# A hybrid decoder layer: AZ as the plain first projection, AV as a seven-product quad, heads of seven blocks

## The chip, the cores and the metric

The kernel runs on one NeuronCore of a Trainium2 chip. The metric is the device time of one execution in microseconds (us). Engines are TensorE (PE; PEld is its weight load), VectorE (DVE), ScalarE (ACT) and SyncE (SP), which here only issues DMAs. GpSimd is not used.

## What is computed

One layer over 512 tokens of width 2048, all in float32:

```python
h = rmsnorm(x, norm_g)
parts = split(h @ w_in)            # w_in: 2048 x 24576 columns in blocks of 1024, and three gates of 2048
aq, ak, av, az = parts[0:4]        # branch A, 8 heads of 2 x 64
# branch A: per head p = softmax(q1 k1) - lam * softmax(q2 k2), o = p @ v, rmsnorm(o)
ya = oa * silu(az)
# branch B: 8 heads, three groups (q, k, v each) with dilation 1, 4, 16, joined by their denominators
yb = ob * silu(bz)
yc = cb * conv3(cc * cx) * silu(cz)
merged = sum(sigmoid(gate_i) * (y_i @ w_branch_i))
out = rmsnorm(x + merged @ w_out, final_g)
```

A product is made in float32 precision by three matmuls: both operands are split into a high part, rounded to the fast format (fp32r), and the rest, and high x high, high x low and low x high are summed in PSUM (`three`, L619).

## The kernel before

**Units and splits.** Weights come in units of 128 x 1024 floats (512 KB). A unit's `w_hi` is made by ScalarE (a copy) and its `w_lo` by VectorE (a subtraction), each in a ring of three (`RING`). TensorE waits for `w_lo` (`lo_done`); ScalarE splits unit n+3 when TensorE has finished unit n (`pe_used`). SyncE loads the raw units into another ring of three.

**Stages in order.** (1) A *plain* projection of 1024 columns, 16 units, with activations held still and weights moving: the values of branch A (AV). (2) Five *quads*, 1 to 5. A quad is a block of 1024 columns by 2048 rows computed with seven products of halves (Strassen's scheme) instead of eight, P1 to P4 in 28 units of 12 matmuls. VectorE adds the halves of the weights (four kinds, `add_units`, four units each) and takes each product's two PSUM banks into `gin` (`take_g`); ScalarE stores the result to `c_dram`. These quads give AQ, AK and the three V of branch B. (3) Eight *heads*, with attention. (4) Quads 6 to 15, branch C and gates, with branch C's convolution beside them. (5) The three branch projections and the output projection, also with seven products, from summed weights in `s_dram`.

**Heads.** Head 0 and head 7 are written out, heads 1 to 6 are a loop of three heads that runs twice (`Fori`, on each engine). A head has eight projection blocks, w = 2 to 9: Q0, K0, Q1, K1, Q2, K2, AZ, BZ. Each is 128 columns, two units of 24 matmuls (8 chunks of K x 3), with weights held still. The result lies in one of three banks `proj`, and VectorE scales it by the tokens' root (`scale_block`). AQ and AK of the head come from `c_dram` and are turned by TensorE into such a bank. Between the units, TensorE does attention: `scores_a`, `scores_b` (into `sc_ps`), `probs_a`, `probs_b` (transposes into `tr_ps`), `values_a`, `values_b` (into `o_ps`) and `squares_a` (sum of squares for branch A's norm). A step of softmax goes through the engines: scores (PE), `bias` with the minimum (DVE), `exps` (ACT), `norm` (DVE), `probs` (PE), `turned` (high part ACT, low part DVE). Branch A has four such steps in a head (0 to 3), branch B four (0 to 3), of which B's last three fall into the next head's first blocks.

**Sums of branch weights.** 24 times within the heads, ScalarE loads 2 MB of branch or output weights into `ssum` (`load_sums`), VectorE makes four additions (`sum_units`), ScalarE stores 2 MB to `s_dram` (`store_sums`). There is one buffer, so a load waits for the store before. `SUMS_FIRST` and `SUMS_LOOP` give the units at which they are loaded; the sum is two units later, the store three.

**What sets the order.** Everything is written out by hand: each engine's program calls the same steps in its own order, in `blocks` (PE), two functions `head` (ACT and DVE) and the loops over quads. Every engine takes its instructions in order, so a wait holds up all behind it.

```python
def bank(self, b):
    return (NBLK1 * self.k + ENTRY[b]) % RING
```

## Time and profile before

| | |
|---|---|
| time, median of 3 runs (lowest, highest) | 2504.5 us (2504.45, 2504.55) |
| the profiled execution's own time | 2505.15 us |
| its span, first to last instruction | 2503.4 us |
| mean granted clock of TensorE | 0.999 |
| busy: PE, PEld, DVE, ACT | 2484.4, 2053.7, 1945.7, 1069.8 us |
| matmuls | 11454 |
| read from and written to HBM | 420.64 MB, 96.47 MB |

Busy time is the union of an engine's instructions. Matmuls overlap, so the printed mean of one is longer than the distance between two starts. "Idle before, releaser" is the time in which an engine did nothing before an instruction, and what the profile takes to have ended it; "issue" means that it waited for nothing the profile shows. Times in timelines are counted from the first instruction.

### The profile page before, as it was taken

How to read it: one execution, taken by the hardware profiler on the slowest of the kernel's cores; microseconds unless marked ns; L12 is line 12 of the kernel's file. 1: busy time of each engine (PE TensorE's matmuls, PEld its weight loads, DVE VectorE, ACT ScalarE, POOL GpSimd, SP SyncE). 2: the span in 40 equal slices, each digit the busy share in tenths (PEclk: the TensorE clock that was granted, in tenths of full speed). 3: DMA queues.
4: the chain of work that ended last, by engine and by line, in shares of the span. 5: the costliest groups of instructions: out<-in, count | busy, mean ns of one | idle time of the engine just before them, and what ended most of it. 6: DMA issues, size and time to landing. Idle time of an engine off the chain costs nothing.

```text
span 2503.4 us, 30481 instructions
## 1 busy us (share of the span) xinstructions
PE 2484.4 (99%) x11454; PEld 2053.7 (82%) x11454; DVE 1945.7 (78%) x2266; ACT 1069.8 (43%) x1329; POOL 0.2 (0%) x4
## 2 busy tenths in 40 slices
PE   9999999999999999999999999999999999999998
PEld 8888888888888888888887788888878888788887
DVE  8797788566676767767678887788878888898875
ACT  5343333334333333333434433344444445655644
POOL 0000000000000000000000000000000000000000
PEclk9999999999999999999999999999999999999999
DMA  8255444686776667766535545445565456787666
GB/s 317 95 198 188 150 133 143 203 301 214 252 266 231 223 213 248 264 234 225 191 106 193 203 168 193 170 154 193 181 218 203 160 197 219 261 286 247 226 227 202
DMA packets 184902, 519.15 MB, mean 207 GB/s; under 512 B 14129, under 2 KB 59442, under 8 KB 181042
## 3 DMA queue, kind: packets, MB, share of 16 engines
q1 hardware_dynamic: 87872, 342.62, 39.9%
q10 hardware_dynamic: 96882, 174.55, 19.8%
q8 instruction: 94, 1.54, 0.2%
q14 instruction: 54, 0.44, 0.1%
HBM read 420.64 MB, written 96.47 MB: 207 GB/s over the span
## 4 chain that ended last, share of the span: by engine, by line
PE 92%; DVE 3%; DMA 3%; ACT 1%; issue 1%; DVEq 0%; ACTq 0%
PE proj L621 13%; PE proj L623 13%; PE proj L622 13%; PE sc_ps L621 6%; PE sc_ps L622 6%; PE sc_ps L623 6%; PE tr_ps L621 6%; PE tr_ps L622 6%; PE tr_ps L623 6%; PE o_ps L622 4%; PE o_ps L623 4%; PE o_ps L621 4%; PE tr_ps L664 1%; DVE w_lo L1547 1%; DMA rows<-c_dram 1%; DMA raw<-s_dram 1%
## 5 line engine op out<-in xcount | busy, mean ns | idle before, releaser
L1008 ACT ACTIVATE w_hi<-raw 128x1024 fp32r<-128x1024 f32 x296 | 314.0, 1061 | 430.3 <-PE proj L623 138.1
L1008 ACT ACTIVATE w_hi<-kb 128x1024 fp32r<-128x1024 f32 x280 | 297.2, 1062 | 442.6 <-PE proj L623 156.9
L1547 DVE TENSOR_TENSOR w_lo<-raw,w_hi 128x1024 fp32r<-128x1024 f32 x296 | 361.2, 1223 | 156.2 <-ACT w_hi L1008 155.3
L1547 DVE TENSOR_TENSOR w_lo<-kb,w_hi 128x1024 fp32r<-128x1024 f32 x280 | 342.7, 1224 | 116.6 <-ACT w_hi L1008 116.0
L621 PE MATMUL proj<-act_hi,w_hi 128*128 128x512 f32 x1024 | 405.8, 396 | 1.7 <-DVE w_lo L1591 1.7
L623 PE MATMUL proj<-act_hi,w_lo 128*128 128x512 f32 x1024 | 399.6, 390 | 0.0
L622 PE MATMUL proj<-act_lo,w_hi 128*128 128x512 f32 x1024 | 398.7, 389 | 0.0
L1057 ACT ACTIVATE w_hi<-raw 128x1024 fp32r<-128x1024 f32 x128 | 135.6, 1060 | 344.8 <-PE proj L623 339.9
L1591 DVE TENSOR_TENSOR w_lo<-raw,w_hi 128x1024 fp32r<-128x1024 f32 x128 | 156.6, 1224 | 103.1 <-ACT w_hi L1057 102.6
L623 PEld LDWEIGHTS proj<-act_hi,w_lo 128*128 128x128 f32 x1024 | 192.2, 188 | 41.3
L621 PEld LDWEIGHTS proj<-act_hi,w_hi 128*128 128x128 f32 x1024 | 192.8, 188 | 40.2 <-DVE w_lo L1591 1.9
L622 PEld LDWEIGHTS proj<-act_lo,w_hi 128*128 128x128 f32 x1024 | 192.6, 188 | 38.2
L621 PE MATMUL sc_ps<-w_hi,act_hi 128*128 128x512 f32 x360 | 141.2, 392 | 0.6 <-DVE w_lo L1547 0.5
L621 PE MATMUL tr_ps<-w_hi,act_hi 128*128 128x512 f32 x360 | 140.8, 391 | 0.8 <-DVE w_lo L1547 0.8
L622 PE MATMUL sc_ps<-w_lo,act_hi 128*128 128x512 f32 x360 | 140.2, 389 | 0.0
L622 PE MATMUL tr_ps<-w_lo,act_hi 128*128 128x512 f32 x360 | 140.1, 389 | 0.0
L623 PE MATMUL sc_ps<-w_hi,act_lo 128*128 128x512 f32 x336 | 130.8, 389 | 0.0
L623 PE MATMUL tr_ps<-w_hi,act_lo 128*128 128x512 f32 x336 | 130.8, 389 | 0.0
L621 PE MATMUL tr_ps<-w_hi,tb 128*128 128x512 f32 x328 | 128.4, 392 | 0.6 <-DVE w_lo L1547 0.6
L623 PE MATMUL tr_ps<-w_hi,tb 128*128 128x512 f32 x328 | 127.7, 389 | 0.0
L622 PE MATMUL tr_ps<-w_lo,tb 128*128 128x512 f32 x328 | 127.7, 389 | 0.0
L621 PE MATMUL sc_ps<-w_hi,tb 128*128 128x512 f32 x272 | 106.5, 392 | 1.9 <-DVE w_lo L1547 1.7
(310 smaller groups left out, 4765.1 us busy)
## 6 DMA issues: line engine op xcount, KB each, us to landing
raw<-wg SPq DMA_DIRECT2D x128, 512.0 KB, 3.9
raw<-wst SPq DMA_DIRECT2D x128, 512.0 KB, 4.9
kb<-wg SPq DMA_DIRECT2D x28, 2048.0 KB, 7.6
ssum<-ws ACTq DMA_DIRECT2D x24, 2048.0 KB, 9.3
s_dram<-ssum ACTq DMA_DIRECT2D x24, 2048.0 KB, 7.7
raw<-s_dram SPq DMA_DIRECT2D x96, 512.0 KB, 4.4
raw<-ws SPq DMA_DIRECT2D x72, 512.0 KB, 4.1
kb<-wg SPq DMA_DIRECT2D x56, 512.0 KB, 6.3
```

What stands on the lines that cost most here:

```text
L621: nc.tensor.matmul(out, w_h, a_h, start=first, stop=False, skip_group_check=shared)
L622: nc.tensor.matmul(out, w_h, a_l, start=False, stop=False, skip_group_check=shared)
L623: return nc.tensor.matmul(out, w_l, a_h, start=False, stop=last, skip_group_check=shared)
L664: end = nc.tensor.transpose(tr_ps[idx % 2][:, n * P:(n + 1) * P], tile, ident[:, :])
L1008: nc.scalar.activation(w_hi[r % RING][:, :], src, ACT.Copy).then_inc(hi_done, 1)
L1057: nc.scalar.activation(w_hi[slot][:, :], raw[x][:, :], ACT.Copy).then_inc(hi_done, 1)
L1547: tt(w_lo[r % RING][:, :], src, w_hi[r % RING][:, :].bitcast(f32), ALU.subtract).then_inc(lo_done, 1)
L1591: tt(w_lo[slot][:, :], raw[x][:, :], w_hi[slot][:, :].bitcast(f32), ALU.subtract).then_inc(lo_done, 1)
```

## The change

- The plain projection now computes AZ. Its operands are swapped: weights held still, activations moving, so that a bank holds 128 columns by 512 tokens, the form of a head. It is stored unscaled, one bank per head, to a new `z_dram`, and each head loads its own (`load_z`) into `z_a` and scales it (`scale_z`) in block K2.
- AV becomes one more quad. There are six quads (1 to 6) ahead of the heads, and 7 to 16 behind.
- A head has seven blocks (w = 2 to 8: Q0, K0, Q1, K1, Q2, K2, BZ), 14 units.
- The attention steps move. Scores and transposes now mostly stand between the two units of a block on TensorE, and the transposes of a step come one block after its scores. ScalarE's and VectorE's parts follow. `values_b` of a head stays at the end of K1 in the next head, with `scores_a(1)` ahead and `probs_a(0)` behind it.
- In the last head, steps 2 and 3 of branch B move into the quad after the heads (number 7); that quad uses `o_ps`, `proj0` for the Z chain and `sc_ps` for Y; `values_b` goes to `sc_ps0`, and ScalarE copies `o_ps` to `o_a`.
- Sums of branch weights: one moves into quad 6; in the heads one every four units, with the sum at the end of a block and behind its softmax work.

The core of the diff:

```diff
-NBLK1, NHU1 = 10, 16
+NBLK1, NHU1 = 9, 14
-QUADS_V, QUADS_C, QUADS_G, QUADS_O = 6, 10, 16, 2
+QUADS_V, QUADS_C, QUADS_G, QUADS_O = 7, 11, 17, 2
-SUMS_FIRST = (0, 4, 8, 12)
-SUMS_LOOP = (2, 6, 12, 16, 20, 24, 28, 34, 40, 44)
+SUMS_QUAD, SUM_QUAD_AT = 9, (13, 14, 15, 16)
+SUMS_FIRST = (1, 5, 9)
+SUMS_LOOP = (1, 5, 9, 13, 17, 21, 25, 29, 33, 37)
...
 plain_quad, PE:
-                            ts = slice(P * b, P * (b + 1))
-                            end = three(plain[half][b][:, :], act_hi[:, k, ts], act_lo[:, k, ts], w_hi[slot][:, cs], w_lo[slot][:, cs],
+                            ws = slice(C * kk + P * b, C * kk + P * (b + 1))
+                            end = three(plain[half][b][:, :], w_hi[slot][:, ws], w_lo[slot][:, ws], act_hi[:, k, :], act_lo[:, k, :],
...
 blocks, PE, between the two units of block w:
+                    if w < 5 and not fresh:
+                        scores_b(i - 1, w - 1)
+                    if w == 5:
+                        scores_a(i, 0)
+                    if 6 <= w < 8:
+                        scores_a(i, w - 4)
+                    if w == BZ:
+                        scores_b(i, 0)
+                    if w < 6 and not fresh:
+                        probs_b(i - 1, w - 2)
+                    if 6 <= w:
+                        probs_a(i, w - 5)
                     pe.wait_ge(lo_done, NHU1 * i + (R_H + t + 2))
                     multiply(h.bank(w), h.slot(t + 1), act_hi, act_lo, 8, False, True)
...
+                    if w == 5:
+                        scores_a(i, 1)
+                        if not fresh:
+                            values_b(i - 1, o_ps, (o_free, 2 * i))
+                        probs_a(i, 0)
+                    if w == BZ:
+                        values_a(i)
                         if last:
-                            scores_b(i, 2)
-                        else:
-                            values_a(i)
                             scores_b(i, 1)
                             probs_b(i, 0)
...
 head, DVE, between the two units of block w (behind split(t)), the end of K2 and the end of a block:
+                    if w == BZ:
+                        bias_b(i, 0)
+                        turned_a(i, 3)
+                        low_v(2 * i + 1, v_a)
+                        silu(i, 0, AZ)
+                        norm_b(i, 0)
...
                     scale_block(h, w)
+                    if w == 7:
+                        scale_z(i)
                     split(t + 1)
...
+                    m = h.sums(t + 1, SUM_AT)
+                    if m is not None:
+                        sum_units(m)
...
 after the heads, PE:
                         if n == 1:
-                            scaled(HEADS - 1, AZ)
+                            scaled(HEADS - 1, Q2)
                             squares_a(HEADS - 1, pb[0])
-                            scores_b(HEADS - 1, 3)
+                        if n in (1, 3):
+                            scores_b(HEADS - 1, (n + 3) // 2)
                         if n in (1, 3, 5):
                             probs_b(HEADS - 1, (n + 1) // 2)
                         if n == 7:
-                            values_b(HEADS - 1)
+                            values_b(HEADS - 1, sc_ps[0], (biased, 8 * HEADS + 1))
```

How the instructions stand on VectorE, in head 0, from the end of block K2 on. Before, K2's two units (`w_lo`) close the step 3 of branch A, and the low part of the values (`v_lo`) stands in the block behind, AZ, ahead of everything but one `w_lo`; BZ is still to come:

```order
L1728 SCALAR_TENSOR_TENSOR pr<-sc,rsum,tmp_a 128x512
L1591 TENSOR_TENSOR w_lo<-raw,w_hi 128x1024
L1786 TENSOR_TENSOR v_lo<-v_a,v_hi 128x512
L1704 TENSOR_TENSOR z_a<-proj,rstd 128x512
L1591 TENSOR_TENSOR w_lo<-raw,w_hi 128x1024
L1743 ISA sc,low<-masks,sc_ps 128x512
L1743 ISA low 128x1
L1745 ISA sc,nmax<-masks,sc_ps,low 128x256
L1745 ISA nmax 128x1
L1756 TENSOR_TENSOR pt_lo<-tr_ps,pt_hi 128x4x128
```

Now (from the gate's scaling at the end of K2 into BZ):

```order
L1739 TENSOR_TENSOR z_a<-z_a,rstd 128x512
L1620 TENSOR_TENSOR w_lo<-raw,w_hi 128x1024
L1604 TENSOR_TENSOR ssum<-ssum 128x1024
L1606 TENSOR_TENSOR ssum<-ssum 128x1024
L1608 TENSOR_TENSOR ssum<-ssum 128x1024
L1610 TENSOR_TENSOR ssum<-ssum 128x1024
L1620 TENSOR_TENSOR w_lo<-raw,w_hi 128x1024
L1776 ISA sc,low<-masks,sc_ps 128x512
L1776 ISA low 128x1
L1778 ISA sc,nmax<-masks,sc_ps,low 128x256
L1778 ISA nmax 128x1
L1789 TENSOR_TENSOR pt_lo<-tr_ps,pt_hi 128x4x128
```

The next row there is `v_lo<-v_a,v_hi`: the low part of the values has moved behind the sum of weights, the bias and the transposed probabilities, in the same block at whose end TensorE asks for it.

VectorE in the quad after the heads, units 5 and 6 (each begins with its `w_lo`), before:

```order
L1547 TENSOR_TENSOR w_lo<-raw,w_hi 128x1024
L1756 TENSOR_TENSOR pt_lo<-tr_ps,pt_hi 128x4x128
L1750 RECIPROCAL rsum<-sums 128x1
L1751 TENSOR_SCALAR pr<-sc,rsum 128x768
L1547 TENSOR_TENSOR w_lo<-raw,w_hi 128x1024
L1790 RECIPROCAL tmp_a<-tmp_a 128x512
L1793 SCALAR_TENSOR_TENSOR o_a<-o_ps,gsub,tmp_a 128x512
L1893 TENSOR_SCALAR gin<-proj,rcol 128x512 x2
```

And now:

```order
L1567 TENSOR_TENSOR w_lo<-raw,w_hi 128x1024
L1776 ISA sc,low<-masks,sc_ps 128x512
L1776 ISA low 128x1
L1778 ISA sc,nmax<-masks,sc_ps,low 128x256
L1778 ISA nmax 128x1
L1789 TENSOR_TENSOR pt_lo<-tr_ps,pt_hi 128x4x128
L1783 RECIPROCAL rsum<-sums 128x1
L1784 TENSOR_SCALAR pr<-sc,rsum 128x768
L1567 TENSOR_TENSOR w_lo<-raw,w_hi 128x1024
L1823 RECIPROCAL tmp_a<-tmp_a 128x512
L1830 SCALAR_TENSOR_TENSOR o_a<-o_a,gsub,tmp_a 128x512
L1931 TENSOR_SCALAR gin<-proj,rcol 128x512 x2
```

The bias of step 3 of branch B (two instructions and their minima) has moved from unit 3 to unit 5, ahead of the reciprocal.

## Rows read from the trace of the kernel before

**Rows 1.** The page: busy time, and the granted clock in 40 slices.
```profile
span 2503.4 us, 30481 instructions
PE 2484.4 (99%) x11454; PEld 2053.7 (82%) x11454; DVE 1945.7 (78%) x2266; ACT 1069.8 (43%) x1329; POOL 0.2 (0%) x4
PEclk9999999999999999999999999999999999999999
```

**Rows 2.** One quad: stretch, its length, busy (instructions) per engine, PEclk, DMA share, GB/s.
```profile
200.00:276.20 76.20, 76.20 (x338) 63.13 (x337) 61.53 (x59) 29.77 (x29) 0.00 (x0) 1.00 0.48 165
```

**Rows 3.** The same view, two looped heads.
```profile
580.00:685.40 105.40, 105.40 (x522) 87.51 (x521) 71.45 (x114) 39.70 (x66) 0.00 (x0) 1.00 0.65 228
685.40:790.80 105.40, 105.40 (x522) 87.50 (x521) 74.93 (x115) 38.36 (x65) 0.00 (x0) 1.00 0.73 262
```

**Rows 4.** Timeline of TensorE: quad 5 into head 0; scores of branch B.
```profile
471.64 0.39 PE L621 MATMUL o_ps<-w_hi,tb 128*128 128x512 f32 x1
...
479.80 0.39 PE L621 MATMUL proj<-act_hi,w_hi 128*128 128x512 f32 x1
...
1300.95 0.48 PE L621 MATMUL sc_ps<-qk_hi 128*128 128x512 f32 x1
...
1302.10 0.47 PE L621 MATMUL proj<-act_hi,w_hi 128*128 128x512 f32 x1
```

**Rows 5.** Chain that ended last: `values_b` in four successive heads (start, length).
```profile
732.76 1.78 PE o_ps L712 x16
838.13 1.78 PE o_ps L712 x16
...
945.47 1.78 PE o_ps L712 x16
1050.85 1.78 PE o_ps L712 x16
```

**Rows 6.** Timelines around the loop's jump: TensorE, VectorE, ScalarE.
```profile
892.69 0.82 PE L664 MATMUL tr_ps<-ident,pr 128*128 128x128 f32 x6
895.23 0.49 PE L621 MATMUL proj<-act_hi,w_hi 128*128 128x512 f32 x1 [1.71 <-DVE w_lo L1591]
...
878.43 1.22 DVE L1591 TENSOR_TENSOR w_lo<-raw,w_hi 128x1024 fp32r<-128x1024 f32 x1 [0.40 <-ACT w_hi L1057]
...
902.99 1.06 ACT L1057 ACTIVATE w_hi<-raw 128x1024 fp32r<-128x1024 f32 x1 [4.49 <-issue]
```

**Rows 7.** The sums' loads and stores: ScalarE's timeline, landing (L1042, then L1046), waits.
```profile
866.75 0.40 ACTq L1046 DMA_DIRECT2D s_dram<-ssum  x1
...
874.86 0.41 ACTq L1042 DMA_DIRECT2D ssum<-ws  x1
...
DMA to landing us min/median/max: 8.3/9.3/13.3
...
DMA to landing us min/median/max: 7.0/7.7/9.9
...
DVE ssum L1583 <- DMA ssum<-ws: 4.7, 5, 1.2
```

**Rows 8.** VectorE's groups: count, busy, mean ns of one.
```profile
L1702 DVE TENSOR_TENSOR qk<-proj,rstd 128x512 f32<-128x512 f32 x32 | 34.4, 1075 | 23.4 <-PE proj L623 22.5
L1584 DVE TENSOR_TENSOR ssum<-ssum 128x1024 f32<-128x1024 f32 x24 | 29.4, 1225 | 0.8
L1743 DVE CUSTOM_DVE_ANT_0 sc<-masks,sc_ps 128x512 f32<-128x512 f32 x32 | 21.8, 681 | 0.3 <-DVE pr L1751 0.3
L1745 DVE CUSTOM_DVE_ANT_0 sc<-masks,sc_ps,low 128x256 f32<-128x256 f32 x32 | 15.4, 481 | 6.1 <-DVE low L1743 6.1
```

**Rows 9.** Timelines in quad 6, unit 7: VectorE, then TensorE.
```profile
1336.11 3.35 DVE L1790 RECIPROCAL tmp_a<-tmp_a 128x512 f32<-128x512 f32 x1
...
1341.47 1.22 DVE L1547 TENSOR_TENSOR w_lo<-raw,w_hi 128x1024 fp32r<-128x1024 f32 x1
...
1342.74 0.50 PE L621 MATMUL sc_ps<-w_hi,tb 128*128 128x512 f32 x1 [1.68 <-DVE w_lo L1547]
```

More of the change, by code:

```diff
@@ L708, in values_b @@
                 pe.wait_ge(vg_in, 32 * i + 32)
-                pe.wait_ge(o_free, 2 * i + 2)
+                pe.wait_ge(*free)
                 for g in (1, 2):
                     for c in range(4):
-                        nc.tensor.matmul(o_ps[:, c * P:(c + 1) * P], v_g[g][:, c, :], pt_g[:, g - 1, c, :],
+                        nc.tensor.matmul(bank[:, c * P:(c + 1) * P], v_g[g][:, c, :], pt_g[:, g - 1, c, :],
                                          start=g == 1 and c == 0, stop=False)
@@ L716, in values_b @@
                     bs = slice(32 * n, min(32 * n + 64, P))
-                    end = three(as_class(o_ps[:, :])[:, :, bs], v_hi[:, n, :], v_lo[:, n, :], pt_b[0][:, n, :, bs],
+                    end = three(as_class(bank[:, :])[:, :, bs], v_hi[:, n, :], v_lo[:, n, :], pt_b[0][:, n, :, bs],
                                 pt_b[1][:, n, :, bs], False, n == 3)
@@ L1143, in squares_o @@
                 nc.scalar.activation(sq_hi[:, :], o_ps[:, :], ACT.Square).then_inc(sq_ready, 1)
+                if last:
+                    nc.scalar.activation(o_a[:, :], o_ps[:, :], ACT.Copy).then_inc(o_free, 1)
             def root_o(i, bank):
@@ L1177, in head @@
                         comb_high(6, t2[0], f2, (comb_sum, 6))
-                    if last and w == 9:
-                        squares_o(i)
-                        turned_b(i, 0)
+                    if w < 6 and not fresh:
+                        turned_b(i - 1, w - 2)
+                    if w < 5 and not fresh:
+                        exps_b(i - 1, w - 1)
+                    if 6 <= w:
+                        turned_a(i, w - 5)
+                    if w == 5:
+                        exps_a(i, 0)
+                    if 6 <= w < 8:
+                        exps_a(i, w - 4)
+                    if w == BZ:
+                        exps_b(i, 0)
+                    m = h.sums(t, SAVE_AT)
+                    if m is not None:
+                        store_sums(m)
                     split(t + 1)
@@ L1183, in head @@
                         store_gate(QUADS_V - 1, 2)
+                    if w == 3 and not fresh:
+                        act.wait_ge(vb_in, 16 * i)
+                        act.wait_ge(o_ready, 2 * i - 1)
+                        high_v(v_b)
                     if w == 4:
+                        for b in SPLIT:
+                            split_block(i, b)
                         if fresh:
@@ L1829, in head @@
                         low_turn(h, AQ)
+                        if not fresh:
+                            low_squares(i - 1)
                     if w == K0:
                         low_turn(h, AK)
+                    if w < 5 and not fresh:
+                        bias_b(i - 1, w - 1)
+                        turned_b(i - 1, w - 2)
+                        if w == 4:
+                            inverse_a(i - 1)
+                            norm_o(i - 1)
+                        norm_b(i - 1, w - 1)
@@ new lines, in head @@
+                    if fresh and w == 4:
+                        for n in range(8):
+                            dve.wait_ge(g_stored[n], 16 * QUADS_V)
+                    if w == 5:
+                        bias_a(i, 0, fresh)
+                        if not fresh:
+                            turned_b(i - 1, 3)
+                        norm_a(i, 0)
+                    if 6 <= w < 8:
+                        bias_a(i, w - 4, fresh)
+                        turned_a(i, w - 5)
+                        if w == 6 and not fresh:
+                            join_b(i - 1, o_ps)
+                        norm_a(i, w - 4)
@@ L1841, in head @@
-                    if w == 6 and not fresh:
-                        join_b(i - 1)
-                    if w == 8:
-                        low_v(2 * i + 1, v_a)
-                    if w == 9:
-                        silu(i, 0, AZ)
-                    if last and w == 9:
-                        turned_b(i, 0)
-                        bias_b(i, 1)
                     scale_block(h, w)
+                    if w == 7:
+                        scale_z(i)
                     split(t + 1)
-                    if w < 4 and not fresh:
-                        bias_b(i - 1, w)
@@ new lines, in head @@
+                    if w == 5:
+                        bias_a(i, 1, fresh)
+                        turned_a(i, 0)
+                        if not fresh:
+                            join_a(i - 1)
+                            silu(i - 1, 1, BZ)
+                        norm_a(i, 1)
+                    if last and w == BZ:
+                        bias_b(i, 1)
+                        turned_b(i, 0)
+                        low_squares(i)
+                        norm_b(i, 1)
+                    m = h.sums(t + 1, SUM_AT)
@@ L1875, in take_g @@
+                    if m is not None:
+                        sum_units(m)
             def take_g(q, p):
@@ L1948, in take_plain @@
                 dve.wait_ge(pe_used, RING + UNITS_V // 2 * (half + 1))
[L1949 removed]
+                nc.vector.tensor_copy(gin[:, 4 * half + b, :], plain[half][b][:, :]).then_inc(got, 1)
             def sums_of(q, n):
@@ L2016, in _ @@
             head(fixed(0))
-            links = 3 * (steps["n"] - before - 2 * len(SUMS_FIRST) + 6) + 2 * len(SUMS_LOOP)
+            links = 3 * (steps["n"] - before - 2 * len(SUMS_FIRST) + 7) + 2 * len(SUMS_LOOP)
             with dve.Fori(0, 2) as j:
```

239 lines of the change are left out of this document (100 added, 139 removed).

## The prediction

> **What bounds the kernel now.** I read the page first, then stretches, then single instructions. The page [rows 1] shows TensorE busy 99% of a span of 2503.4 us, its granted clock in the top digit throughout (the 2.4 GHz level), and VectorE at 78%. So TensorE's list of matmuls is the time, and other engines matter only where they make it wait. Stretches of pure projection and of attention differ. A seven-product quad lasts 76.2 us, in which TensorE never idles and VectorE works 61.5 us [rows 2]. A looped head lasts 105.4 us, again without idle TensorE, with VectorE at 71 to 75 us [rows 3]. Some 19 us of the span are idle TensorE (2503.4 less 2484.4).
>
> Matmuls overlap, so the 0.39 us printed for one is not its price; the distance between starts is. In a quad 36 of 128x512 start in 471.64 to 479.80, 0.2267 us each [rows 4], and the change of form there, from activations held still to weights held still, leaves no gap. The same rows print equal durations on both sides. That is the price of every such matmul here: an 8-chunk half block (24) costs 5.44 us, a quad (7 products x 16 x 3 = 336) 76.2 us, as rows 2 measure.
>
> **The sum of the matmuls.** AZ as a head block cost 16 x 3 = 48 matmuls in each of eight heads, 384. It becomes the plain first projection, which is 16 units of 24, 384 too, and takes the slot that AV had. AV now costs a quad, 336. Net 48 fewer: 48 x 0.2267 = **10.9 us less**. In place: eight heads lose 10.9 us each (87.1), one quad adds 76.2. The attention matmuls, transposes and their breaks keep their number. A head should last 105.37 - 10.88 = 94.5 us (period from [rows 5]).
>
> **Work that goes beside it.** The quad adds 28 splits where 16 go, 16 weight additions of about 1.22 us and 7 evictions of two banks on VectorE. The 61.5 us of [rows 2] hold all of these, so they lie in a 76.2 us quad with 14.7 us of VectorE spare: zero; the four additions of a branch-weight sum (4.8 us, [rows 8]) that move into the last quad before the heads fit too, since that quad prepares no successor. Without that spare the 4.8 us would be the price. The plain projection's evictions become copies of the same size: zero. The swapped operands: zero by rows 4. SyncE's weight ring keeps its rule, three units ahead: zero. The gate's load and scaling (one 128x512, under 1.1 us by the scaling of [rows 8]) replace one eviction per head: zero, hidden by the head's spare 20 us of VectorE. The load is one DMA of 256 KB more per head on ScalarE's queue, ahead of a sum's load; it counts below.
>
> **The jump of the loop.** The heads' loop runs three heads twice. The head period is 105.37 us but 107.34 across its jump [rows 5]: 1.97 us. The profile names the residual split (w_lo) as releaser. I don't believe it: TensorE's last transposes start at 892.69, it resumes at 895.23, while the unit it resumes with had its w_lo at 878.43 plus 1.2; and ScalarE, at 902.99, has 4.5 us in which it waited for nothing shown [rows 6]. So I take the gap as the jump itself and leave it: zero, with -2.0 as the other end (were it VectorE's lateness, the new order would remove it) and nothing above, since the number of jumps is the same. The Trainium skill (Runtime: NRT & Kernel Launch, Instruction fetch mechanics) says that a taken branch to a page outside the fetch window has to fetch it before going on. By that rule the 2 us stay and the sum below is 2496.3; by the profile's releaser they would go, and it were 2494.3. The trace agrees with the rule as far as one jump can.
>
> **The tight place in a head.** Softmax steps now stand in mid-block, each a block from the next (first pair of pieces of the order). After its scores (1.15 us, [rows 4]) a step needs a bias of 0.7 + 0.5 [rows 8], an exp and a scaling, each near 1 us, and a w_lo or two stand between: some 6 us, where the transposes ask for it 12 us later. That holds. What doesn't hold so well is block BZ after a block K2 whose end carries a weight sum (sums stand at the end of every second block; in heads 0, 1, 3, 4 and 6 one is at the end of K2). From the end of K2, VectorE: scaling K2 1.0 and the gate 0.6, w_lo 1.1 (from 1.6 on), the sum 4.8, w_lo 1.1, bias 1.3, transposed probabilities 0.6, low part of v_a 0.6: 11.3 us with the small waits. TensorE asks for that low part at the end of BZ, 5.44 + 1.15 + 0.35 + 5.44 = 12.4 us. Slack 1.1 us, if the sum's data are in. That depends on the sum before, at the end of K1: VectorE's small steps there take about 7.4 us and the sum 4.8, of which 4.4 lie beside TensorE's attention, so it ends 7.8 us into Q2; w_lo, bias and exp follow (3.5), and the store goes out at 11.3 of Q2's 12.4 us. It lands 7.7 later, ScalarE issues the next load at once (866.75 and 874.86 show that distance), and that lands after 9.3 [rows 7]: with K2's 12.7 us gone, 3.6 us into BZ, where VectorE is ready at 2.8. So the slack falls to 0.3 us. One load took 13.3 and one store 9.9; with both a head stalls 4.0 + 2.2 - 0.3 = 5.9 us. Ends: 0 and 5.9 us per head. The medians give no stall and a part of the loads is later, so I take 0.3 for each of five heads, **+1.5 us**, close to the medians of rows 7. ScalarE meanwhile waits for the store with the next split queued behind it, 1.2 us late against three units of lead: nothing. Elsewhere (Q1, where the 3.35 us reciprocal [rows 9] meets a sum in heads 2 and 5) I count a surplus of about 3.5 us against some 8 us that the ring of three units gives: zero, at most 1.4 each.
>
> **The seam to the seventh quad.** Here before, TensorE lost 1.7 us: the reciprocal (3.35), the normalization and two evictions ran before w_lo of unit 7 at 1341.47 [rows 9]. The change puts scores and bias 3 between units 3 and 5 instead of earlier. TensorE then reaches unit 7 later by 1.2 us (scores), the reciprocal starts about 2.2 later (bias 1.3 plus the exp chain behind it): **+1.1 us**, ends 0 and 2.5. The second pair of pieces of the order shows what stands ahead of that reciprocal. The new copy of o_ps on ScalarE is under 1 us, hidden by the four units before P5; if not, it costs itself. The rest of that quad rests on the same transfers: zero.
>
> **Sum.** The profiled execution took 2505.15 us, span 2503.4 and 1.75 around it; it lies 0.65 above the median of the three runs. 2505.15 - 10.9 + 0 + 1.5 + 1.1 = 2496.9; against the median 2504.5 - 8.2 = **2496.3 us**, 0.33% less. The measurement can tell about 0.2% (5 us) from no change.
>
> **Rivals.**
> 1. *All of it arrives.* The load lands by its median, the slacks hold, the seam costs nothing: 2504.5 - 10.9 = 2493.6, with the jump's gap gone 2491.6. For: TensorE was never idle in a looped head but at the jump. Against: VectorE already waited for these loads five times [rows 7], when the need was no earlier than now. Chance 0.33.
> 2. *The weight sums become the wait (the slower side).* Mechanism: at the end of K2 VectorE, in order, stands at the sum for its load, and the low part of v_a is queued behind it. A head stalls by what store and load together exceed 17.3 us (7.7 + 9.3 + 0.3). At 2.0 us per head the gain is gone (5 x 2.0 + 1.1), at 3.0 the kernel is 5 us slower; with every load at 13.3 us it is 3.7 per head, 18.5 in all: 2504.5 - 10.9 + 18.5 + 1.1 = 2513.2. For: loads are now issued behind more work, beside y_a, v_b and the gate's load. Against: only a few of 24 loads can have been near 13.3. Chance 0.07 of slower, and 0.15 that it or an overfull VectorE takes 4 to 14 us and leaves 2499.5 to 2509.5 (within 0.2%).
> 3. *The new quad isn't free.* VectorE's spare there is used up by the moved sum: at most 4.8 us, 2501.1. Rows 2 speak against it; inside the 0.15.
>
> **Numbers.** Forecast (2494 to 2499.5) 0.45; all of it 0.33; within 0.2% 0.15; slower 0.07. Faster 0.78, same 0.15, slower 0.07. Range: the low end takes most of rival 1 (the full saving, 0.6 below it for errors in my small terms, not the jump's 2), 2493; the high end takes half of the middle case, 2501.5.
>
> **What the new profile would show.** Quads and plain units as before, 76.2 us each, heads starting 76.2 us later; looped heads 94.5 us apart, plus up to 1 where a sum ends K2; about 2 us more across the jump, which decides between my reading and w_lo; a gap of 2.5 to 3 us before unit 7 of the seventh quad. I am wrong if quads 1 to 6 show idle TensorE, if heads are over 96.5 us apart, or if values of branch A (o_ps) wait for v_lo by more than 1 us in a head. Should the heads be 94.5 with no waits, rival 1 has it.

## The result, and the profile after

The change makes the kernel slower: 2524.7 us (median of 4, 2521.1 to 2525.9) against 2504.5 of the kernel before in the same job (4 runs), ratio 1.0078, 95% interval 1.0066 to 1.0091. The forecast was 2496.3, in a range of 2493.0 to 2501.5.

The page of the changed kernel (its profiled execution took 2524.84 us), against [rows 1]:

```profile
span 2522.9 us, 30435 instructions
PE 2484.2 (98%) x11406; PEld 2049.8 (81%) x11406; DVE 1981.1 (79%) x2308; ACT 1082.6 (43%) x1342; POOL 0.2 (0%) x4
```

The 48 matmuls are gone (11454 to 11406), but TensorE's busy time is the same (2484.4, now 2484.2) and its idle time has doubled, from 19.0 to 38.7 us. The same stretch of one quad as in [rows 2]:

```profile
200.00:276.20 76.20, 76.20 (x338) 63.13 (x337) 61.55 (x60) 29.72 (x28) 0.00 (x0) 1.00 0.48 166
```

It is as before: TensorE is never idle in these 76.2 us. The chain that ended last shows where the time goes: `values_b` in successive heads (start, length), as [rows 5].

```profile
697.96 1.98 PE o_ps L716 x16
...
893.15 1.98 PE o_ps L716 x16
...
996.03 1.98 PE o_ps L716 x16
...
1095.82 2.05 PE o_ps L716 x16
...
1193.01 1.98 PE o_ps L716 x16
...
1289.03 1.98 PE o_ps L716 x16
```

Two heads take 195.2 us, then one 102.9 (across the jump), 99.8, 97.2 and 96.0, where 94.5 was forecast. Waits of ScalarE, VectorE and TensorE in the changed kernel (us in total, times, longest):

```profile
ACT w_hi L1065 <- DMA s_dram<-ssum: 65.0, 13, 6.8
ACT L1163 <- DMA s_dram<-ssum: 10.4, 2, 5.3
DVE ssum L1604 <- DMA ssum<-ws: 9.7, 7, 2.6
PE o_ps L625 <- DVE v_lo L1819: 7.5, 5, 3.1
PE proj L647 <- ACT tmp_a L1163: 4.9, 2, 2.5
PE proj L625 <- issue: 3.9, 1, 3.9
PE o_ps L625 <- DVE pt_lo L1789: 1.9, 1, 1.9
```

The four rows of PE are 18.2 us of new idle time in looped and first heads (only the jump's 1.7 was there before). Behind some of the gaps the granted clock came down. Windows of 4 us around the jump and around the 3.1 us gap (columns as in [rows 2]):

```profile
936.00:940.00 4.00, 0.67 (x7) 0.53 (x5) 1.67 (x2) 1.09 (x2) 0.00 (x0) 0.98 1.04 389
940.00:944.00 4.00, 3.47 (x8) 2.81 (x9) 0.00 (x0) 0.00 (x0) 0.00 (x0) 0.50 0.61 200
944.00:948.00 4.00, 4.00 (x13) 3.11 (x13) 0.00 (x0) 0.00 (x0) 0.00 (x0) 0.67 0.00 0
...
1036.00:1040.00 4.00, 0.90 (x4) 0.50 (x3) 3.77 (x9) 1.82 (x3) 0.00 (x0) 0.85 0.46 136
1040.00:1044.00 4.00, 4.00 (x18) 3.60 (x17) 2.50 (x4) 1.25 (x3) 0.00 (x0) 0.72 1.00 409
```

PEclk 0.50 is the 1.2 GHz level; matmuls start 0.43 us apart there instead of 0.23. Over the nine such windows of the changed kernel before its end the missing clock, (1 - PEclk) x 4 us each, is 8.6 us, which counts as busy time. The kernel before has none, except at its very end. So the account is -10.9 (matmuls) + 16.5 (gaps in the heads) + 1.0 (seam) + 8.6 (clock) = 15.2 of the 19.5 us by which the span grew. Of the other 4.3, 2.2 are idle time outside these rows (idle time grew by 19.7 in all) and 2.1 are busy time; what that busy time is was not worked out.

### The profile page after: what moved, and what is told of

It reads as the page before. It is cut to its first block, busy times and chain, and to the rows that moved or that the text cites. A ratio compares the mean times of both kernels' runs of the same rounds, so it can differ in the third digit from the quotient of the medians.

```text
span 2522.9 us, 30435 instructions
## 1 busy us (share of the span) xinstructions
PE 2484.2 (98%) x11406; PEld 2049.8 (81%) x11406; DVE 1981.1 (79%) x2308; ACT 1082.6 (43%) x1342; POOL 0.2 (0%) x4
## 4 chain that ended last, share of the span: by engine, by line
PE 79%; DMA 9%; DVE 8%; issue 3%; ACT 1%; ACTq 0%; DVEq 0%
PE proj L625 9%; PE proj L627 8%; PE proj L626 8%; PE sc_ps L625 7%; PE sc_ps L626 6%; PE sc_ps L627 6%; PE tr_ps L625 6%; PE tr_ps L626 6%; PE tr_ps L627 6%; PE o_ps L625 4%; PE o_ps L626 4%; PE o_ps L627 4%; DMA s_dram<-ssum 4%; DMA ssum<-ws 3%; DVE w_lo L1567 1%
## 5 line engine op out<-in xcount | busy, mean ns | idle before, releaser
L1016 ACT ACTIVATE w_hi<-kb 128x1024 fp32r<-128x1024 f32 x300 | 318.1, 1061 | 474.1 <-PE proj L627 162.3
L1567 DVE TENSOR_TENSOR w_lo<-kb,w_hi 128x1024 fp32r<-128x1024 f32 x300 | 366.9, 1223 | 122.5 <-ACT w_hi L1016 121.9
L625 PE MATMUL proj<-act_hi,w_hi 128*128 128x512 f32 x944 | 376.3, 399 | 3.9 <-issue 3.9
L627 PE MATMUL proj<-act_hi,w_lo 128*128 128x512 f32 x944 | 369.9, 392 | 0.0
L626 PE MATMUL proj<-act_lo,w_hi 128*128 128x512 f32 x944 | 369.4, 391 | 0.0
L625 PEld LDWEIGHTS proj<-act_hi,w_hi 128*128 128x128 f32 x944 | 178.6, 189 | 39.1 <-issue 4.0
L627 PEld LDWEIGHTS proj<-act_hi,w_lo 128*128 128x128 f32 x944 | 178.1, 189 | 38.4
L626 PEld LDWEIGHTS proj<-act_lo,w_hi 128*128 128x128 f32 x944 | 178.6, 189 | 35.4
L625 PE MATMUL tr_ps<-w_hi,tb 128*128 128x512 f32 x344 | 134.4, 391 | 0.0
L627 PE MATMUL tr_ps<-w_hi,tb 128*128 128x512 f32 x344 | 134.0, 390 | 0.0
L1089 ACT ACTIVATE sc<-sc,nmax 128x768 f32<-128x768 f32 (+4 forms) x96 | 65.5, 683 | 119.1 <-DVE nmax L1778 59.9
```

The costliest lines, as they stand in the source:

```text
L625: nc.tensor.matmul(out, w_h, a_h, start=first, stop=False, skip_group_check=shared)
L626: nc.tensor.matmul(out, w_h, a_l, start=False, stop=False, skip_group_check=shared)
L627: return nc.tensor.matmul(out, w_l, a_h, start=False, stop=last, skip_group_check=shared)
L1016: nc.scalar.activation(w_hi[r % RING][:, :], src, ACT.Copy).then_inc(hi_done, 1)
L1089: end = nc.scalar.activation(tile[:, lo:hi], tile[:, lo:hi], ACT.Exp, scale=-1.0, bias=nmax[:, m:m + 1], accum_out=sums[:, m:m + 1])
L1567: tt(w_lo[r % RING][:, :], src, w_hi[r % RING][:, :].bitcast(f32), ALU.subtract).then_inc(lo_done, 1)
```

## How one head goes wrong

The head with the longest gap, around the end of K2. ScalarE's store and load of a sum:

```profile
1009.98 0.40 ACTq L1054 DMA_DIRECT2D s_dram<-ssum  x1
...
1018.73 0.39 ACTq L1050 DMA_DIRECT2D ssum<-ws  x1
```

VectorE, from the split that waited for ScalarE to the low part of the values:

```profile
1020.34 1.23 DVE L1620 TENSOR_TENSOR w_lo<-raw,w_hi 128x1024 fp32r<-128x1024 f32 x1 [5.87 <-ACT w_hi L1065]
1021.48 0.68 DVE L1751 CUSTOM_DVE_ANT_0 sc<-masks,sc_ps 128x512 f32<-128x512 f32 x1
...
1027.52 1.22 DVE L1620 TENSOR_TENSOR w_lo<-raw,w_hi 128x1024 fp32r<-128x1024 f32 x1
1030.84 1.23 DVE L1604 TENSOR_TENSOR ssum<-ssum 128x1024 f32<-128x1024 f32 x1 [2.10 <-DMA ssum<-ws]
...
1038.67 0.68 DVE L1819 TENSOR_TENSOR v_lo<-v_a,v_hi 128x512 fp32r<-128x512 f32 x1
```

TensorE:

```profile
1035.92 0.39 PE L627 MATMUL proj<-act_hi,w_lo 128*128 128x512 f32 x1
1039.40 0.80 PE L625 MATMUL o_ps<-pt_hi,v_hi 128*128 128x512 f32 x1 [3.10 <-DVE v_lo L1819]
```

The forecast had the store out 11.3 us into Q2, which is 1010.1 here, counted back from the values' due time: right (1009.98). The load follows 8.75 later (the forecast's timeline took 8.1, its rule 7.7), and its data are in at 1030.84, 12.1 after its issue (9.3 was taken). The forecast's rule, a stall of what store and load together exceed 17.3 us, gives 8.75 + 12.1 - 17.3 = 3.6; TensorE waited 3.1. In the three other looped heads with a sum there it gives 1.4 to 2.0 and TensorE waited 1.0 to 1.2. In the whole kernel the landings are these, of the loads and of the stores (min, median, max; [rows 7] had 9.3 and 7.7):

```profile
DMA to landing us min/median/max: 7.8/9.6/12.7
...
DMA to landing us min/median/max: 7.0/8.5/11.2
```

The second thing to see is the first row of VectorE. ScalarE stood for the store's landing until 1018.73, with the copy w_hi of the next unit behind it; so w_lo came 5.9 us later than VectorE was free, and the bias of the softmax step stands behind w_lo. TensorE didn't need that unit yet. VectorE's order made the bias need it. In this head that delay was made up (VectorE stood idle for the load afterwards, 2.10 us). In head 2, where no sum stands at the end of K2, it reached TensorE by itself:

```profile
831.02 1.06 ACT L1065 ACTIVATE w_hi<-raw 128x1024 fp32r<-128x1024 f32 x1 [2.26 <-DMA s_dram<-ssum]
...
832.11 1.23 DVE L1620 TENSOR_TENSOR w_lo<-raw,w_hi 128x1024 fp32r<-128x1024 f32 x1 [4.54 <-ACT w_hi L1065]
...
835.88 0.50 PE L625 MATMUL o_ps<-pt_hi,v_hi 128*128 128x512 f32 x1 [1.08 <-DVE v_lo L1819]
```

In head 0 (TensorE's wait of 1.9 us on `pt_lo`) VectorE didn't wait for the sum's load either; one w_lo in K2 had made it stand 5.2 us for ScalarE, whose copy came behind the store's landing (2.1 us in q1_own_queue, where ScalarE has no store to wait for).

## Experiments

**The sums left out, whole or in part.** Three kernels from the changed one, one from the kernel before. The stage behind reads unsummed weights of the same size in all of them (in e3_transfers_only what was stored back unsummed).

```diff
 e1_no_sums, b1_no_sums:
             def load_sums(m):
+                return
             def store_sums(m):
+                return
-                for step in range(4):
-                    sum_unit(m, step)
 e1_no_sums, b1_no_sums, e2_adds_only:
-                load_ring(x, (s_dram if summed_ else ws)[i, kind, :, :])
+                load_ring(x, ws[i, kind, :, :])
 e2_adds_only, in the heads:
-                        load_sums(m)
-                        store_sums(m)
 e3_transfers_only, in the heads:
-                for step in range(4):
-                    sum_unit(m, step)
+                dve.wait_ge(osum_in, 16 * (m + 1))
+                dve.sem_inc(osum_done, 1)
```

> The changed kernel without the 24 sums of branch and output weights: their loads, additions and stores are left out, and the projections behind read the unsummed weights in the same amount. Kernel before 2504.5 us, changed kernel 2524.7 us. Theory S (the sums are what stalls TensorE in the seven-block heads, and the lowered clock follows from those stalls): the six waits of branch A's values at the end of BZ and the two for the root at K0 vanish, the only gaps left are the loop's jump and the seam after the heads, mean granted clock 0.999; 2504.5 - 10.9 + 1 for the seam, 2493 to 2498 us. Rival T (the new order of attention is too tight by itself): gaps before branch A's values stay at 1 us or more per head, at least 2508 us. Rival Q (the added quad or the swapped projection cost): time lost before 557 us, not seen so far, at least 2504 us.

Measured: 2494.9 (2492.2 to 2500.6), ratio 0.9968 (0.9956 to 0.9979). The sums are the whole loss: without them the change brings 9.1 us of the 10.9. The chain's rows of `values_b`:

```profile
692.67 1.98 PE o_ps L716 x16
...
787.18 1.98 PE o_ps L716 x16
...
881.69 1.98 PE o_ps L716 x16
...
977.02 1.98 PE o_ps L716 x16
...
1071.54 1.98 PE o_ps L716 x16
```

94.51 us per head, as forecast, and 95.33 across the jump.

> The changed kernel with all additions of the sums on VectorE at their places, but with one load and one store in the last quad only: the 23 transfers within the heads are left out, and the additions repeat on the same data. Theory S1 (the round trip store, load, sum through one buffer is what is late, through ScalarE's wait for the store and VectorE's wait for the load): gaps before branch A's values below 0.3 us each, as in the kernel without sums, 2494 to 2500 us. Rival S2 (the 4.8 us of additions in VectorE's queue are late by themselves): the gaps of about 1 us before branch A's values stay, the waits for the root vanish, 2503 to 2512 us.

Measured: 2497.0, 0.9973 (0.9963 to 0.9984). VectorE does every addition, 1983.1 us busy, and TensorE waits for none of them. VectorE isn't overfull.

> The changed kernel with all loads and stores of the sums and all their waits on both engines, but without the additions in the heads (23 x 4 instructions on VectorE are left out). Theory S1: the round trip loses its 4.8 us of additions and 3 to 4 us of waiting, so store and load fit in two blocks; between the kernel without sums and the changed kernel, 2495 to 2503 us, with ScalarE still waiting for stores. Theory S2: the same as without sums, 2493 to 2498 us. If the waits for transfers alone hold everything up (theory S3), 2510 us or more and gaps before the values as in the changed kernel.

Measured: 2506.1 (2503.5 to 2507.5), 1.0005 (0.9995 to 1.0014). This lies between the bands of theories S1 and S3, so neither number held. The time rose by 11 us with no addition in the heads: 0.6 and 0.7 us of TensorE on `tmp_a`, where ScalarE waits for a store ahead of a root, and a jump of 4.2 us with the clock at 1.2 GHz behind it. From the last turn of AK on the profiled execution was also 7 us longer than that of e1_no_sums (1270.6 against 1263.2 us), though no sum is transferred there any more: 3.4 us are a lower clock behind the seam and at 1860, and TensorE's gaps there come to 11.3 us against 6.7. Why is open, so not all of the 11 us is shown to be the transfers' doing.

> The kernel before without its 24 sums (loads, additions and stores left out, the projections read the unsummed weights). TensorE had no gap in its heads but at the loop's jump. Theory J (the gap at the jump is the jump): it stays at 1.5 to 2 us and the time is the kernel before's within 1 us, 2503.5 to 2505. Rival W (the gap was VectorE's late split, as the profile names it, behind a sum that waited for its load): it goes, 2501.5 to 2503.

Measured: 2504.2, 0.9997 (0.9987 to 1.0006). The old order carries the same 24 sums for nothing.

**Is it the density?** The kernel before with its sums four units apart:

```diff
-SUMS_LOOP = (2, 6, 12, 16, 20, 24, 28, 34, 40, 44)
+SUMS_LOOP = (2, 6, 10, 14, 18, 22, 26, 30, 34, 38)
```

> The kernel before with its ten sums in three looped heads at one every four units (as the changed kernel has them) instead of 4, 4 and 6 apart; nothing else. It asks whether the density alone costs, or the density together with the new order. Theory S1 with the order (the old order has the low part of the values a whole block ahead of its use and heads 10.9 us longer): little, 2503 to 2508. Rival D (a cycle of store, load and sum of about 22 us can't keep a distance of four units in any order): waits on v_lo or tmp_a in most looped heads, 2512 or more.

Measured: 2507.5, 1.0013 (1.0004 to 1.0022). Four waits on `tmp_a` of 0.6 us, none on the values. Density alone costs 3 us (1 to 5.5 by the interval). The rest then comes with what else the change did: the new order, the shorter head, and what is in flight at the jump.

**Other places for the sums.** A second sum in quad 6, nine instead of ten in three looped heads, none at the end of K2 or K0. The second kernel also moves the reciprocal at the seam, the third does only that.

```diff
 p1_placed, p2_placed_seam:
-SUMS_QUAD, SUM_QUAD_AT = 9, (13, 14, 15, 16)
-SUMS_LOOP = (1, 5, 9, 13, 17, 21, 25, 29, 33, 37)
+SUMS_QUAD, SUM_QUAD_AT = (9, 20), ((13, 14, 15, 16), (23, 24, 25, 26))
+SUMS_LOOP = (-1, 3, 7, 13, 17, 21, 27, 31, 35, 41)
 p2_placed_seam, s1_seam:
-                        if n == 6:
+                        if n == 12:
                             inverse_a(HEADS - 1)
```

> The changed kernel with the same 24 sums, placed otherwise: a second one into quad 6, nine in three looped heads instead of ten, only at the ends of Q0, K1 and Q2, none at the end of K2 or of K0, two of three 4 units apart and the third 6. Nothing is left out. Theory S1 (round trip of store, load and addition that leaves no slack at a distance of four units, and what is queued behind it on VectorE and ScalarE): no wait of TensorE on v_lo or on tmp_a is left in the heads, the clock dips that follow them go too, and the time is that of the kernel without sums plus the loop's jump: 2495 to 2499. Rival Q (density: nine sums in three heads still fill VectorE or the queues): waits of 1 us and more stay, 2506 or more. A load of 2 MB goes out at the jump here; if code loading waits for such traffic, the jump's gap stays above 1.5 us.

Measured: 2505.0 (2499.8 to 2508.0), 0.9998 (0.9989 to 1.0007). The forecast of 2495 to 2499 was missed: the waits on `v_lo` and `tmp_a` are gone and 20 us with them, but not 28. TensorE now waits 2.1 us at the start of the heads, 1.2 at the jump, and about 0.4 to 0.9 per head in small pieces. The jump's gap of 1.2 us is below the 1.5 that its expectation set for theory J2; the section on the jump says why.

> As p1_placed, and in quad 7 the reciprocal and the normalization of branch A go from unit 6 to unit 12. If the reciprocal (3.35 us) ahead of w_lo of unit 7 is what makes the gap of 2.6 us at the seam, the gap falls under 0.5 us: 1.5 to 2.5 us less than p1_placed, more (up to 4) where the clock fell behind that gap: 2492 to 2497, below both kernels. Rival: the later reciprocal makes another split late at unit 13 or holds back y_a: no less than p1_placed.

Measured: 2506.2, 1.0004 (0.9995 to 1.0013).

> The changed kernel with the reciprocal and the normalization of branch A at unit 12 of quad 7 instead of unit 6, nothing else. By the same reason as in p2_placed_seam the gap of 2.63 us before unit 7 goes, and with it the stretch at a granted clock of 0.61 behind it: 2519 to 2523. Rival (the reciprocal only moves the wait to unit 13): 2524 or more.

Measured: 2526.0 (2522.1 to 2532.6), 1.0087 (1.0072 to 1.0102). Both miss: the gap of 2.63 us before unit 7 is gone, but 1.65 us come before unit 13 and smaller ones behind them. The reciprocal only moves the wait, as the rival said.

**The start of the heads and the jump.** `p3_jump_free` packs quad 6's sums closer and `p4_start` doesn't; both move loads behind the jump.

```diff
 p3_jump_free:
+SUMS_QUAD, SUM_QUAD_AT = (9, 18), ((13, 13, 14, 14), (22, 22, 23, 23))
 p3_jump_free (heads 1, 4, 7) and p4_start (0, 1, 4, 7): in the middle of Q0, not ahead of it
+                    if w == Q0 and h.k in (0, 1, HEADS - 1):
+                        load_sums(h.sums(1, SUM_AT))
```

> As p1_placed, with two repairs. The two sums of quad 6 are packed closer (two additions in one unit, the second sum loaded at unit 18), so that the store before the third load has landed when ScalarE comes to it: in p1_placed ScalarE stood there, the third w_hi of the heads came late and TensorE lost 2.1 us at 564.48 (3.6 us with what hangs on it). And the load that went out at the loop's jump goes out in the first unit behind it. If both readings are right: no gap at the first turn of AQ, the jump's gap at 0.5 to 0.9 us as in e1_no_sums, 4 to 5 us less than p1_placed: 2499 to 2502, a little under before. If the jump's gap stays at 1.2 us and more with no transfer of a sum in flight, theory J2 (code loading waits for bulk traffic) is wrong; if the start of the heads is as late as in p1_placed, VectorE, not ScalarE's wait, made it late.

Measured: 2506.5, 1.0010 (1.0001 to 1.0019). A miss: two additions in one unit made `w_lo` late in quad 6 (gaps of 1.1 and 1.9 us), and the jump's gap was 1.9 us without a sum in flight. By the test in its expectation that spoke against theory J2; it doesn't, as the timing of the code packets below shows.

> As p1_placed (the two sums of quad 6 spaced as there, not packed), but the first load in head 0 and the load at the loop's jump go out in the middle of block Q0 instead of ahead of it. It asks whether ScalarE's wait for the store, ahead of a split that TensorE's start of the heads needs, is what made that start late in p1_placed (2.09 us at 564.48, 3.6 with what hangs on it). If so the gap at the first turn of AQ is under 0.5 us and the jump's gap is near 1 us: 3 to 4 us less than p1_placed, 2501 to 2502.5, 0.1% under before, which the measurement can just not tell. If the start is as late as before, VectorE's additions in units 23 to 26 made it late, and the time is 2505 or more.

Measured: 2507.2, 1.0009 (1.0000 to 1.0017). A miss too: the start is as late as before (2.05 us). ScalarE's timeline there:

```profile
550.93 1.06 ACT L1016 ACTIVATE w_hi<-raw 128x1024 fp32r<-128x1024 f32 x1 [4.22 <-DMA raw<-wg]
550.94 0.39 ACTq L1054 DMA_DIRECT2D s_dram<-ssum  x1
...
560.22 1.06 ACT L1065 ACTIVATE w_hi<-raw 128x1024 fp32r<-128x1024 f32 x1 [4.62 <-DMA raw<-wst]
```

Neither of my two explanations holds. ScalarE waits for raw weights: the DMA engines are full (share 1.0 from 545 to 562), and the loads raw<-wst issued there land after 6.9 us (median), against 4.6 in the changed kernel, which has no second sum there. That points to the sum's traffic; no run takes the traffic away and leaves the rest.

**One store at the jump.** The changed kernel, in which the store that is in flight at the jump carries 256 bytes (the expectation calls it a few KB), and the stage behind reads unsummed weights:

```diff
 store_sums, for the last sum of three looped heads:
+                    act.dma_start(s_dram[bass.ds(m, 1), :, 0:1, 0:16].rearrange("o t p q -> p (o t) q"), ssum[0:1, :, 0:16]).then_inc(osum_stored, 16)
```

> The changed kernel in which one store of a sum, the last of three looped heads (2 MB, in flight while the engines jump back), carries a few KB only; the stage behind reads unsummed weights of the same size, so the output is another. Theory J2 (the code behind the jump is fetched through the same DMA engines and waits for bulk traffic): the gap at the jump falls from 3.85 us to under 1.5, the stretch at half clock behind it goes, and the time falls by 5 to 8 us to 2517 to 2520. Rival J (the gap is the jump's own, or its code's): it stays near 3.9 us and the time within 1 us of 2524.7.

Measured: 2523.2 (2510.9 to 2527.1), 1.0071 (1.0047 to 1.0095). The gap fell from 3.85 to 1.6 us, but the clock came down at another gap just ahead of it (2.6 us on `v_lo`), and the time hardly changed. The total doesn't decide; the gap itself does, with the packets below.

**The transfers on a queue of their own.** GpSimd, idle so far, issues all 24 loads and stores; ScalarE neither issues nor waits.

```diff
+        @block.gpsimd
+        def _(gp):
+            gp.wait_ge(pe_used, RING + first_unit(QUADS_V - 1) + 2 * NU)
+            for m in range(SUMMED):
+                if m:
+                    gp.wait_ge(osum_stored, 16 * m)
+                gp.dma_start(ssum[:, :, :], ws[m:m + 1, ...]).then_inc(osum_in, 16)
+                gp.wait_ge(osum_done, m + 1)
+                gp.dma_start(s_dram[m:m + 1, ...], ssum[:, :, :]).then_inc(osum_stored, 16)
```

> The changed kernel in which GpSimd, idle so far, issues the 24 loads and stores of the sums from a program of its own, each as soon as what it waits for is there; ScalarE issues none and waits for none. VectorE's additions stay where they are. Nothing is left out. Theory A (ScalarE's wait for a store, with the split of weights queued behind it, is what makes VectorE's small steps late): the waits of w_lo on w_hi in the heads fall back, the gaps on v_lo, pt_lo and tmp_a go, 2524.7 falls to 2497 to 2503. Rival B (the data themselves come too late and the traffic is in the way, whoever issues it): gaps of 1 us and more stay at the ends of the value blocks, 2510 or more. The distance from store to load can't shrink by more than a few tenths of a us, since the load waits for the landing in both.

Measured: 2513.3 (2509.7 to 2515.6), 1.0032 (1.0020 to 1.0045): 11.4 us less than the changed kernel, with VectorE's work and the sums' places as they were, but not the 2497 to 2503 of theory A. Its waits and the jump:

```profile
PE proj L625 <- issue: 5.1, 1, 5.1
PE o_ps L625 <- DVE v_lo L1830: 3.5, 4, 1.3
...
929.36 0.27 PE L627 MATMUL o_ps<-pt_hi,v_lo 128*128 128x128 f32 x1
934.77 0.79 PE L625 MATMUL proj<-act_hi,w_hi 128*128 128x512 f32 x1 [5.15 <-issue]
```

The waits on `tmp_a` are gone, as A said, and those on `v_lo` halved. But the jump got longer (5.15 us), head 0's wait on `pt_lo` too (2.7 us for 1.9; VectorE stood 3.7 us for the sum's load there), and gaps of about 1 us stay: the late data of rival B are real as well.

> As q1_own_queue, with the places of p1_placed (two sums in quad 6, spaced 4, 4 and 6 units in the heads). Loads go out as soon as the store before has landed, so they are early everywhere, and none is tied to the loop's jump. Theory A: 2495 to 2500, below the kernel before. Rival B: within 2 us of p1_placed's 2505.

Measured: 2512.7, 1.0032 (1.0020 to 1.0044), a miss, 7.7 above p1_placed. Early loads are no gift: 3.8 us at the start of the heads, 1.3 twice in head 0, 3.9 at the jump.

**And the store held back at the jump, head 0's third sum moved.**

```diff
 q3_hold, q4_hold_bz:
+                if m == len(SUMS_FIRST) + len(SUMS_LOOP):
+                    gp.wait_ge(pe_used, NHU1 * 4 + R_H + RING + 1)
 q4_hold_bz:
-SUMS_FIRST = (1, 5, 9)
+SUMS_FIRST = (1, 5, 11)
```

> As q1_own_queue, and GpSimd holds back one store, the one that was in flight while the engines jump back in the loop, until TensorE has finished the first unit behind the jump. Theory J2 (code behind the jump comes late while 2 MB are in flight): the jump's gap falls from 5.2 us to 0.5 to 2, the stretch at 1.2 GHz behind it goes or shortens: 5 to 7 us less than q1_own_queue, 2506 to 2508. Rival J (the gap is the jump's own): 2513 as q1_own_queue.

Measured: 2507.0 (2503.1 to 2510.9), 1.0015 (1.0006 to 1.0024): 6.3 us less than q1_own_queue, for the time at which one store goes out.

> As q3_hold, with the third sum of head 0 at the end of BZ instead of K2. If the sum at the end of K2 is what makes the gap of 2.7 us at head 0's values of branch A, the gap goes: 2 to 3.5 us less than q3_hold, 2503 to 2505.5, as the kernel before. Rival (the next sum, then four units behind it, only moves the wait on): no less than q3_hold.

Measured: 2503.9 (2501.7 to 2508.4), 1.0002 (0.9993 to 1.0011). Here is the changed kernel, complete, 21 us faster by who issues the transfers, when one store goes out and where one sum stands. This and q3_hold came out as expected. It equals the kernel before. None of the full kernels I tried is faster than that one by more than the measurement can tell. q4_hold_bz still has 0.5 us on the values in three heads and 2.2 at the jump.

Windows of 1 us in the jump's gap, of q1_own_queue and then of q3_hold:

```profile
930.60:931.60 1.00, 0.00 (x0) 0.00 (x0) 0.04 (x1) 0.21 (x1) 0.00 (x0) 1.00 1.00 414
931.60:932.60 1.00, 0.00 (x0) 0.00 (x0) 0.00 (x0) 0.00 (x0) 0.00 (x0) 1.00 1.03 410
```

```profile
934.40:935.40 1.00, 0.08 (x1) 0.00 (x0) 1.00 (x1) 0.82 (x2) 0.00 (x0) 1.00 0.03 8
935.40:936.40 1.00, 0.18 (x1) 0.18 (x2) 0.09 (x1) 0.26 (x1) 0.00 (x0) 1.00 0.03 8
```

The last column but one is the DMA engines' share: full in the one, idle in the other.

**The jump, packet by packet.** The traces record TensorE's branch instruction and the DMA queues that carry code. All packets in the changed kernel's gap (936.67 to 940.53), and the one of the code queue q8 among them; then the same for e1_no_sums, 921.0 to 924.3:

```profile
DMA packets 338, 1.40 MB, mean 362 GB/s; under 512 B 1, under 2 KB 1, under 8 KB 336
...
q8 instruction: 1, 0.02, 1.5%
```

```profile
DMA packets 2, 0.02 MB, mean 7 GB/s; under 512 B 0, under 2 KB 0, under 8 KB 0
...
q8 instruction: 1, 0.02, 2.0%
```

In each of the 17 kernels the first q8 packet behind the branch has 16 KB, takes 0.9 to 1.4 us, and ends 1.7 us (1.66 to 1.76) before TensorE's first matmul behind the jump. What differs is when it starts. All times in us, counted from the branch instruction; the last column is the DMA engines' share in the second us behind it, when the packet is due:

| kernel | gap of TensorE | packet starts | TensorE resumes | matmuls still ran for | DMA share |
|---|---|---|---|---|---|
| e1_no_sums, p4_start, e2_adds_only | 0.5, 0.6, 0.8 | 1.0 | 3.8, 3.6, 3.6 | 3.3, 3.0, 2.9 | 0.1 to 0.2 |
| b2_dense, p1_placed, b1_no_sums, p2_placed_seam | 1.2, 1.2, 1.4, 1.6 | 1.0 to 1.2 | 3.6 to 4.0 | 2.4 to 2.6 | 0.0 to 0.2 |
| e4_small_store, before, q3_hold | 1.6, 1.7, 1.7 | 1.0 | 4.1, 4.1, 3.7 | 2.5, 2.4, 1.9 | 0.0 |
| p3_jump_free, q4_hold_bz | 1.9, 2.2 | 1.0 | 4.2, 4.2 | 2.3, 1.9 | 0.3, 0.0 |
| changed kernel | 3.9 | 3.2 | 5.8 | 2.0 | 1.0 |
| q2_own_queue_placed, e3_transfers_only | 3.9, 4.2 | 3.7, 4.8 | 6.5, 7.4 | 2.6, 3.3 | 1.0 |
| s1_seam, q1_own_queue | 4.3, 5.2 | 4.4, 4.5 | 7.0, 7.1 | 2.7, 2.0 | 1.0, 0.95 |

So the gap is the time until the code is there, less the matmuls that had been issued before the branch. With the DMA engines full the packet starts 2 to 4 us later, and that is nearly the whole difference between gaps of 0.5 to 2.2 us and of 3.9 us and more; among the short gaps it is mostly the matmuls already issued that differ. q1_own_queue and q3_hold differ in one store's time alone (packet at 4.5 and at 1.0 us). In p1_placed and p2_placed_seam the sum's load goes out 1.8 us behind the start of that packet; there TensorE stops once more inside the first unit, for 0.7 and for 2.9 us (p2_placed_seam, the fifteenth matmul behind the jump):

```profile
939.88 0.39 PE L627 MATMUL proj<-act_hi,w_lo 128*128 128x512 f32 x1 [2.89 <-issue]
```

The Trainium skill (Runtime: NRT & Kernel Launch, Instruction fetch mechanics) says that an engine's sequencer fetches code by a DMA queue of its own, and that a branch to a page outside its window waits for that; the traces agree, by the packets above.

## Why the prediction was wrong, step by step

- *The sum of the matmuls, -10.9 us*: right. Heads are 94.51 us apart in e1_no_sums (94.5 forecast), and 9.1 us arrive there, seam and start included.
- *The quad, the plain projection, the swapped operands, the gate: zero*: right for the quads (76.2 us, no idle). The sum that moves into quad 6 costs TensorE no gap; the start of the heads is 1.6 us later than in e1_no_sums, of which 1.1 us arose in the first 10 us of the program.
- *The seam, +1.1*: right. The gap went from 1.68 to 2.63 us. The 1.7 us of clock behind it belong to the last point.
- *The jump stays, nothing above it*: this failed. "The number of jumps is the same" says nothing of what is in flight at one. The changed order puts a store of 2 MB there; the packet of code starts 2.2 us later, and the jump costs 2.1 us more, and 5 to 6 with the clock behind it. That the old gap was no matter of w_lo holds: in the kernel before TensorE resumes 1.7 us behind the packet of code, as in all the others.
- *The sums at the end of K2, +1.5*: place and rule were right, the sizes failed. I took medians of the kernel before for transfers that now meet other traffic. In the four looped heads where VectorE waited there, store and load took 18.7 to 20.9 us against 17.3, and TensorE waited 6.4 us in all (1.0, 1.1, 3.1, 1.2). The rule also had a slip: the timeline takes 8.1 us from the store to the next load, the rule 7.7. With 8.1 in both (17.7) it gives 1.0, 1.4, 3.1 and 1.5.
- *"ScalarE meanwhile waits for the store with the next split queued behind it: nothing"*: this is the step that was worth most, and it was false. I compared the late split with TensorE's lead of three units. But VectorE runs its half of the split ahead of the bias, in order, so the delay went into the softmax steps; heads 2 and 0 show it reaching TensorE (1.1 and 1.9 us). The split was not 1.2 us late: 65 us of ScalarE's waits, 13 of 5.0 us on average, stood behind that "nothing". Taking them off gave back 11.4 us in all (q1_own_queue), with the waits below and their clock.
- *Elsewhere zero*: this failed as well. ScalarE's root for the turn of AK stands behind such a wait at two K0 (4.9 us), and the 1.1 us of head 2 have no sum at the end of K2.
- *The clock* didn't occur in the prediction: 8.6 us in the profiled execution.

Rival 2 was the right rival, in mechanism and place, and its ceiling of 2513 was too low, because it held only one of the three ways by which the sums' transfers reach TensorE. Its chance of 0.07 rested on "only a few of 24 loads can have been near 13.3". A cycle with 0.3 us of slack in five heads deserved more.

## What to carry to other kernels

An instruction that waits isn't free because its own engine has slack: go through what stands behind it on that engine, and then through what stands behind *that* on the engines that consume it. Where an order is tightened, take the duration of a transfer from its slow end and not from its median, since the same change moves it among other traffic. Long transfers belong on a queue on which nothing else waits, and away from a loop's jump: code comes by the same DMA engines (1.0 us from branch to packet, or 3.2 to 4.8 when they were full).

## What the runs showed of the hardware

A gap of TensorE may cost more than itself. Behind a single gap of up to 1.7 us no stretch below the full 2.4 GHz was seen; behind two of 0.9 and 1.3 us, 0.6 us apart, there was one (p4_start). Behind the same gap of 2.63 us at the seam the clock came down in eight kernels of twelve and stayed up in four: the changed kernel lost 1.7 us of clock there, e1_no_sums nothing. Two gaps of 2.3 and 2.5 us in the changed kernel left it up, one of 1.85 brought it down. The Trainium skill (TensorE: Matmul & The Clock Gate, Part 1: The HAM clock gate) describes two levels of the clock that follow TensorE's activity; the rows agree, matmuls of 512 columns start 0.43 or 0.23 us apart. Single executions of a kernel with such gaps scatter, and their mean granted clock goes with it: in e4_small_store 2510.9 us at 0.998, and 2526.9 and 2527.1 at 0.994 and 0.995, where the kernel before stays within some 8 us at 0.999. What decides whether the clock falls behind a given gap stays open.
